# First expert's rows from two sources: an early gather of four tiles and a one-hot product from SBUF for the last, with the second gate weights loaded at another point

## The chip, the core and the metric

One core of a Trainium2 chip runs the whole program, one inference step of a decoder layer. The metric is the device time of one execution in microseconds. Inputs lie in HBM in float32, and all products are float32.

## What is computed

The reference computes one layer: RMSNorm and one input projection, two mixers side by side (gated MLP over chunks, and sparse attention with three branches), output projection with residual, then a mixture of 16 experts with residual, and a final RMSNorm. There are 512 prompt tokens and 32 sampled ones (544 rows of width 1024). The change touches the start of the experts:

```python
def _hier_moe(x, ...):                       # x: 544 x 1024, after norm2
    lg = x @ w_rg + b_rg                     # 4 groups of experts
    grp = argmax(lg); g_gate = softmax(lg)[grp]
    le = (x @ w_re + b_re) of that group     # 4 experts in it
    top_p, top_i = top_k(softmax(le), 2)     # two experts for each token
    w = g_gate * top_p / sum(top_p)
    for e in range(16):                      # hidden width 512
        h = silu(x @ w_gate[e]) * (x @ w_up[e])
        y = y + combine[:, e:e+1] * (h @ w_down[e])
    return y
```

An expert has 2 MB of gate, 2 MB of up and 2 MB of down weights, so the experts read 96 MB of weights.

## The kernel before

The program is written out by hand: one instruction list per engine (SyncE, TensorE, ScalarE, VectorE, GpSimd), ordered among each other by named semaphores. An engine takes its list strictly in order, so a wait holds all that stands behind it. Most DMAs are issued by SyncE; gathers and scatters by row index (`indirect_dma_start`) and the stores of rows by GpSimd.

**Output product and router.** The 544 rows are five tiles, taken in `ORDER` = 0, 1, 2, 4, 3 (tile 4 is the 32 sampled rows), so step r = 4 (`PT`) is a full tile of 128 rows and comes last. For each step r: `out_product(r, 0/1)` on TensorE, `residual` on VectorE gives `x2`, `rows_in_columns` turns x2 for the router, `router_parts` and `router_sum` give the logits, `chosen_of(r)` on VectorE finds the two experts (`oh` is the one-hot over experts), `positions(r)` on TensorE counts with a triangular matrix which place in its expert each token takes, `placed(r)` turns this into `in_slot`, and `tokens_in_slots(r)` accumulates in PSUM bank 1, for every expert and slot, the number of the token that sits there. Meanwhile GpSimd multiplies x2 by the norm vector into `h2` (`times_vector`, two halves), ScalarE scales it by the row's norm (`normed`), and GpSimd stores it to the HBM table `scratch_h2` (`rows_stored`, L2838) and x2 to `scratch_x3` (`raw_rows_stored`, L2821).

**Start of the experts.** After step 4, `fixed_tokens` (L2498) makes the index column of experts 0 and 1. GpSimd's `gathered(n)` (L2860) fetches the rows of expert n from `scratch_h2` into `xe[n % 2]`. TensorE's `turn_of(n)` (L1441) turns them with eight transposes into PSUM banks 0 and 1; `rows_out(n)` copies them as columns to `xeT` (ScalarE L1857 half of them, VectorE L2582 the other half); `first_of(n)` does gate and up products, `last_of(n)` the down product. Experts 0 and 1 are fixed (64 and 128 places). The other 14 are sorted by their number of tokens: `experts_weighed` (L2504) and `experts_ranked` (L2513) on VectorE write `expert_at`, from which SyncE reads which expert's weights to load third, fourth and so on (`placed`). `weights_ready` counts up to 2 when the mixing weights are there; TensorE waits for it (L1234) ahead of the experts.

**Weights.** SyncE issues them in a fixed order (L605 to L666). Gate weights go in turn to three slots, up weights to three, down weights to three; a slot is loaded again when the product that used it is counted (`g_mm`, `u_mm`, `y_mm`). Gate 0, up 0, up 1, down 0 and down 1 are loaded before the experts begin. Gate 1 goes to ring slot 4, which holds the first half of the output weights until `out_mm` counts ten. Gate 2 goes to `xr`, which holds x2, and up 2 to `tabs`, which holds h2; both have to be free first. The lines are:

```python
            sp.wait_ge(sem("out_mm"), 2 * TILES)              # L614
            gate_in_turn(1, 1)
            sp.wait_ge(sem("x2_out"), 16 * (TILES + 1))
            sp.wait_ge(sem("experts_placed"), 1)
            placed = {FIXED: expert_of(FIXED)}
            sp.wait_ge(sem("xe_in0"), 16)                     # L624
            gate_in_turn(placed[2], 2)
```

In the trace, L692 is the helper through which all matmuls go, L469 the helper of SyncE's loads.

## Time and profile before

| | before |
|---|---|
| median of three runs | 717.05 us (714.43 to 718.75) |
| profiled execution | 716.05 us, span 714.4 us |
| TensorE matmul busy | 659.5 us, 92% |
| VectorE / ScalarE / GpSimd busy | 264.0 / 188.8 / 156.3 us |
| DMA over the span | 185.61 MB, 260 GB/s |
| granted TensorE clock, mean | 0.982 |

The page gives the busy share of each engine in 40 slices of 17.9 us each (one digit is tenths, 9 is 90% or more), and under them the granted TensorE clock and the data rate:

```profile
PE   4999999999999788989999958999999999889786
POOL 0405007230143086500032411011211111201000
PEclk9999999999999999999999987999999999999999
DMA  9995238153479086602497249999999999999973
```

The experts begin in the 25th slice (from 428.6 us): from there DMA stands at 9 for fourteen slices. In the 24th TensorE has its 5, its lowest digit after the first slice, and the granted clock has an 8 and a 7 in the 24th and 25th. The change lies at this place.

### The profile page before, as it was taken

The page shows a single profiled execution, that of the slowest core. Times are in us where ns is not written, and L with a number is a line of the kernel's source. Part 1 is how long each engine was busy: PE and PEld are TensorE (multiplying, and loading weights), DVE is VectorE, ACT ScalarE, POOL GpSimd, SP SyncE. Part 2 cuts the span into 40 slices and gives each one's busy share as a digit, 9 for nine tenths or more (in the row PEclk, how much of TensorE's full clock was granted, in tenths as well). Part 3 has the DMA queues.
Part 4 walks back from the last instruction along what each step waited for, and adds up shares of the span by engine and source line. Part 5 has one row for each costly group of instructions (what it writes and reads, how often), then busy time and mean ns, then how long its engine had stood idle before and what let it go on. Part 6 is the DMA issues. An engine that isn't in the chain of part 4 may idle for free.

```text
span 714.4 us, 14840 instructions
## 1 busy us (share of the span) xinstructions
PE 659.5 (92%) x5468; PEld 420.1 (59%) x5468; DVE 264.0 (37%) x818; ACT 188.8 (26%) x465; POOL 156.3 (22%) x237
## 2 busy tenths in 40 slices
PE   4999999999999788989999958999999999889786
PEld 1476497847646355557555435865686856456432
DVE  4148220137435666765244862112111011101216
ACT  4110212212132883576333321011111010101104
POOL 0405007230143086500032411011211111201000
PEclk9999999999999999999999987999999999999999
DMA  9995238153479086602497249999999999999973
GB/s 334 380 338 189 78 128 297 46 193 119 147 234 357 38 216 165 211 1 86 154 427 301 93 177 313 403 370 395 377 371 411 354 389 379 365 380 386 368 287 136
DMA packets 56786, 185.61 MB, mean 260 GB/s; under 512 B 9021, under 2 KB 30814, under 8 KB 50562
## 3 DMA queue, kind: packets, MB, share of 16 engines
q1 hardware_dynamic: 44914, 152.54, 56.8%
q0 software_dynamic: 11792, 32.05, 14.7%
q8 instruction: 45, 0.74, 0.4%
q14 instruction: 35, 0.29, 0.1%
HBM read 172.57 MB, written 13.93 MB: 261 GB/s over the span
## 4 chain that ended last, share of the span: by engine, by line
PE 74%; DMA 14%; DVE 5%; ACT 2%; issue 2%; SPq 1%; DVEq 0%; POOLq 0%; ACTq 0%
PE ps L692 68%; DMA ring<-in_w_gate_dram 6%; DMA ring<-in_w_up_dram 5%; PE ps L941 2%; PE ps L1241 1%; SPq L429 1%; DMA ring<-in_w_in_dram 1%; DMA ring<-in_cmp_pages_dram 1%; DMA h_rows<-tabs 1%; PE ps L788 1%; PE ps L968 1%; PE ps L1114 1%; ACT tabs L1682 1%; DMA ugr<-h_rows,qbd 1%; PE ps L1045 0%
## 5 line engine op out<-in xcount | busy, mean ns | idle before, releaser
L692 PE MATMUL ps<-ring,xr 128*128 128x512 f32 (+3 forms) x640 | 140.2, 416 | 9.7 <-DMA ring<-in_w_in_dram 9.7
L692 PEld LDWEIGHTS ps<-ring,xr 128*128 128x128 f32 (+1 forms) x640 | 68.9, 152 | 73.9 <-issue 60.8
L692 PE MATMUL ps<-ring,vnr 128*32 128x128 f32 (+1 forms) x1152 | 79.8, 328 | 2.6 <-DMA ring<-in_w_gate_dram 1.5
L692 PE MATMUL ps<-ring,work 128*32 128x128 f32 (+2 forms) x512 | 71.6, 369 | 0.0
L429 POOL DMA_DIRECT2D ring<-in_sel_pages_dram x96 | 51.4, 536 | 92.2 <-issue 57.0
L692 PEld LDWEIGHTS ps<-ring,vnr 128*32 128x32 f32 (+1 forms) x1152 | 54.6, 124 | 27.7 <-issue 10.6
L2878 POOL DMA_INDIRECT x_rows<-kvn,qbd x14 | 20.6, 1469 | 199.9 <-DVE kvn L2638 60.8
L2582 DVE COPY vnr<-ps 128x256 f32<-128x256 f32 (+3 forms) x16 | 8.1, 508 | 141.9 <-PE ps L1241 141.9
L692 PE MATMUL ps<-ring 128*128 128x128 f32 (+1 forms) x512 | 60.2, 279 | 0.2 <-DMA ring<-in_cmp_pages_dram 0.2
L692 PEld LDWEIGHTS ps<-ring 128*128 128x128 f32 x512 | 59.1, 191 | 0.7 <-DMA ring<-in_cmp_pages_dram 0.4
L692 PE MATMUL ps<-ring,qT 128*32 128x256 f32 (+2 forms) x320 | 52.8, 490 | 4.4 <-DMA ring<-in_w_down_dram 3.7
L429 POOL DMA_DIRECT2D ring<-in_cmp_pages_dram x64 | 34.7, 542 | 80.6 <-PE ps L692 53.9
L692 PEld LDWEIGHTS ps<-ring,work 128*32 128x32 f32 (+1 forms) x512 | 33.6, 130 | 26.0 <-issue 24.6
L1682 ACT ACTIVATE tabs<-tabs,rt 128x128 f32<-128x128 f32 (+3 forms) x64 | 35.2, 555 | 19.6 <-DVE rt L2097 19.5
L692 PEld LDWEIGHTS ps<-ring,qT 128*32 128x32 f32 (+2 forms) x320 | 19.9, 128 | 31.0 <-issue 27.2
L2097 DVE CUSTOM_DVE_ANT_0 tabs<-ps,tabs 128x128 f32<-128x128 f32 (+3 forms) x64 | 28.1, 488 | 14.7 <-PE ps L692 13.9
L1857 ACT COPY vnr<-ps 128x256 f32<-128x256 f32 (+3 forms) x16 | 7.0, 439 | 85.1 <-PE ps L1241 85.1
L941 PEld LDWEIGHTS ps<-cst,tabs 128*128 128x128 f32 x160 | 17.2, 141 | 12.0 <-issue 7.2
L941 PE MATMUL ps<-cst,tabs 128*128 128x128 f32 x160 | 22.1, 279 | 1.8 <-ACT xr L1692 0.9
L692 PE MATMUL ps<-xr,kvn 128*64 128x128 f32 (+2 forms) x264 | 22.3, 303 | 0.3 <-DVE xr L2200 0.3
L692 PE MATMUL ps<-vnr,ring 128*128 128x128 f32 x192 | 21.8, 275 | 0.0
L692 PEld LDWEIGHTS ps<-vnr,ring 128*128 128x128 f32 x192 | 21.6, 192 | 0.0
(404 smaller groups left out, 833.4 us busy)
## 6 DMA issues: line engine op xcount, KB each, us to landing
ring<-in_w_gate_dram SPq DMA_DIRECT2D x11, 2048.0 KB, 25.5
ring<-in_w_down_dram SPq DMA_DIRECT2D x10, 2048.0 KB, 30.2
ring<-in_w_up_dram SPq DMA_DIRECT2D x9, 2048.0 KB
xr<-in_w_gate_dram SPq DMA_DIRECT2D x5, 2048.0 KB, 31.8
tabs<-in_w_up_dram SPq DMA_DIRECT2D x5, 2048.0 KB, 34.2
ring<-in_cmp_pages_dram SPq DMA_DIRECT2D x64, 128.0 KB, 5.0
ring<-in_cmp_pages_dram POOLq DMA_DIRECT2D x64, 128.0 KB, 5.3
ring<-in_w_in_dram SPq DMA_DIRECT2D x3, 2048.0 KB, 9.0
```

Source lines behind the costliest of these rows:

```text
L429: eng.dma_start(dst[:, 256 * j + part.start:256 * j + part.stop], table[bass.ds(page, 1), :, part].rearrange("o p n -> (o p) n")).then_inc ...
L692: return nc.tensor.matmul(out, lhsT, rhs, start=start, stop=stop)
L788: ins = nc.tensor.transpose(bank[:, 128 * m:128 * m + rows], src, ident[0:rows, 0:rows])
L941: ins = nc.tensor.transpose(pb[4 + g][:, at:at + P], prob[s % 3][:, g, n * k + P * m:n * k + P * m + P], ident)
L968: ins = nc.tensor.transpose(pb[7][:, P * h:P * h + P], oT[pair % 2][:, P * h:P * h + P], ident)
L1114: ins = nc.tensor.transpose(pb[2 + h][:, P * k:P * k + rows], x2[0:rows, i, W * h + P * k:W * h + P * k + P], ident[0:rows, 0:rows])
L1241: ins = nc.tensor.transpose(pb[k // 4][:, P * (k % 4):P * (k % 4) + cap], xe[par][0:cap, P * k:P * k + P], ident[0:cap, 0:cap])
L1682: A(v, v, ACT.Exp, scale=-1.0, bias=rt[:, 160 + u % 32:161 + u % 32], accum_out=rt[:, total:total + 1]).then_inc(sem("probs"), 1)
L1857: nc.scalar.copy(xeT[par][:, 0:4, 0:cap], pb[0][:, :].rearrange("p (k n) -> p k n", k=4)[:, :, 0:cap]).then_inc(sem("xt_ready"), 1)
L2097: return V.tensor_tensor_reduce(out, a, b, scale, 3.0e38, ALU.add, ALU.min, acc)
L2582: V.tensor_copy(xeT[par][:, 4:8, 0:cap], pb[1][:, :].rearrange("p (k n) -> p k n", k=4)[:, :, 0:cap]).then_inc(sem("xt_ready"), 1)
L2878: po.indirect_dma_start(scratch_x3, bass.IndirectOffsetOnAxis(slot_tokens[0:cap, n:n + 1].bitcast(U32), 0), ye[n % 2][0:cap, :], None, com ...
```

## The change

The rows of expert 0 are no longer fetched after all five steps. The token numbers of the first four steps are closed in PSUM before the last (`first_earlier` on VectorE), and GpSimd gathers these rows between its two multiplies of the last step (`first_gathered`). Slots that are empty so far stay zero; a further store writes zeros into the rows of the last tile in `scratch_h2` beforehand. On TensorE, eight products with the identity put the gathered rows as columns into banks 0 and 4 (`first_rows_gathered`), and eight products of the last tile's `h2`, still in SBUF, with a one-hot of its slots (`first_here`) add the rest (`first_rows_here`). They take the place of `turn_of(0)`. The counts of the last step move to bank 5. On VectorE, `rows_out(0)` now comes ahead of `experts_ranked`, which comes ahead of `fixed_tokens`, and one addition joins the two parts of the token table. On SyncE, gate 1 waits for the router sum of step 3, which TensorE does amid the last output product, and gate 2 no longer for `xe_in0`; up 2 waits for `xt_mm`, the count of the joined products.

```diff
+        first_here = rt[:, 372:372 + LIGHT_CAP]
+        first_found = ints[:, 28:29]
...
+        def place_counts(r):
+
+            return pb[5][:, 0:E] if r == PT else pb[6][:, E * r:E * r + E]
...
-            sp.wait_ge(sem("out_mm"), 2 * TILES)
+            sp.wait_ge(sem("logit_mm"), 2 * PT)
             gate_in_turn(1, 1)
-            sp.wait_ge(sem("x2_out"), 16 * (TILES + 1))
+            sp.wait_ge(sem("x2_out"), 16 * (TILES + 2))
             sp.wait_ge(sem("experts_placed"), 1)
...
             placed = {FIXED: expert_of(FIXED)}
-            sp.wait_ge(sem("xe_in0"), 16)
-            gate_in_turn(placed[2], 2)
             sp.wait_ge(sem("logit_mm"), 2 * TILES - 1)
             for k in range(2):
                 sp.wait_ge(sem("h2_out%d" % k), 16 * (3 - k))
+            gate_in_turn(placed[2], 2)
+            sp.wait_ge(sem("xt_mm"), 1)
             up_in_turn(placed[2], 2)
...
             def positions(r):
 
                 after(te, "in_slot", r)
+                if r:
+                    mm(place_counts(r), ones, run, True, False)
                 if r == PT:
-                    mm(pb[6][:, E * r:E * r + 2 * E].rearrange("p (k e) -> p k e", e=E), ones,
-                       run[:, None, :].to_broadcast([P, 2, E]), True, False)
-                elif r:
-                    mm(pb[6][:, E * r:E * r + E], ones, run, True, False)
+                    mm(counts, ones, run, True, False)
                 te.wait_ge(sem("onehot_ready"), r + 1)
-                ins = mm(pb[6][:, E * r:E * r + E], cst[:, C_TRI:C_TRI + P], oh[:, r, :], r == 0, r < PT)
+                mm(place_counts(r), cst[:, C_TRI:C_TRI + P], oh[:, r, :], r == 0, True).then_inc(sem("pos_mm"), 1)
                 if r == PT:
-                    ins = mm(pb[6][:, E * TILES:E * TILES + E], ones, oh[:, r, :], False, True)
-                ins.then_inc(sem("pos_mm"), 1)
+                    mm(counts, ones, oh[:, r, :], False, True).then_inc(sem("pos_mm"), 1)
...
             out_product(4, 0)
             out_product(4, 1)
+            tokens_in_slots(3)
             rows_in_columns(4, 1)
             router_parts(4)
-            tokens_in_slots(3)
             router_sum(4)
+
+            def first_bank(k):
+
+                return pb[4 * (k // 4)][:, LIGHT_CAP * (k % 4):LIGHT_CAP * (k % 4 + 1)]
+
+            def first_rows_gathered():
+
+                te.wait_ge(sem("xe_in0"), 16)
+                for k in range(KD):
+                    mm(first_bank(k), xe[0][0:LIGHT_CAP, P * k:P * k + P], ident[0:LIGHT_CAP, 0:LIGHT_CAP], k % 4 == 0, False)
+
+            def first_rows_here():
+
+                te.wait_ge(sem("h2_ready"), 2 * TILES)
+                te.wait_ge(sem("in_slot"), TILES)
+                for k in range(KD):
+                    ins = mm(first_bank(k), h2[0][:, P * k:P * k + P], first_here, False, k % 4 == 3)
+                ins.then_inc(sem("xt_mm"), 1)
+
             positions(4)
+            first_rows_gathered()
+            first_rows_here()
             tokens_in_slots(4)
             te.wait_ge(sem("weights_ready"), 2)
...
-            turn_of(0)
             first_of(0)
             turn_of(1)
             weights_in_slots()
...
+                if n == 0:
+                    nc.scalar.copy(xeT[0][:, 0:4, 0:cap], pb[0][:, 0:4 * cap].rearrange("p (k n) -> p k n", k=4)
+                                   ).then_inc(sem("xt_ready"), 1)
+                    return
...
+            def first_earlier():
+
+                dve.wait_ge(sem("slot_mm"), 1)
+                link(V.tensor_scalar(nowhere[:, 0:1], pb[1][0:CAP, 0:1], 0.0, empty_row[0:CAP, :], ALU.is_equal, ALU.mult))
+                V.scalar_tensor_tensor(out=first_found, in0=nowhere[:, 0:1], scalar=-1.0, in1=pb[1][0:CAP, 0:1],
+                                       op0=ALU.add, op1=ALU.add).then_inc(sem("part_out"), 1)
+
+            def first_last():
+
+                dve.wait_ge(sem("pos_mm"), TILES)
+                V.scalar_tensor_tensor(out=first_here, in0=slot_row[:, 0:LIGHT_CAP], scalar=place_counts(PT)[:, 0:1],
+                                       in1=oh[:, PT, 0:1].to_broadcast([P, LIGHT_CAP]), op0=ALU.is_equal, op1=ALU.mult
+                                       ).then_inc(sem("in_slot"), 1)
 
...
             residual(4, 1)
+            first_earlier()
             columns_out(4)
             norm_of(4)
             parts_out(4)
             chosen_of(4)
             dve.sem_inc(sem("weights_ready"), 1)
+            first_last()
             placed(4)
...
             def fixed_tokens():
 
-                dve.wait_ge(sem("slot_mm"), 1)
-                tokens_from(pb[1][0:CAP, 0:FIXED], slot_tokens[0:CAP, 0:FIXED], 1)
+                dve.wait_ge(sem("slot_mm"), 2)
                 link(V.tensor_copy(found_rows, pb[1][:, 0:E]))
+                link(V.tensor_tensor(found_rows, found_rows, pb[1][:, E:2 * E], ALU.add))
+                tokens_from(found_rows[0:CAP, 0:FIXED], slot_tokens[0:CAP, 0:FIXED], 1)
 
             def experts_weighed():
 
                 n = E - FIXED
+                dve.wait_ge(sem("pos_mm"), TILES + 1)
                 link(V.scalar_tensor_tensor(out=count_key, in0=cst[:, C_IE + FIXED:C_IE + E], scalar=-1.0 / 32,
...
             experts_weighed()
+            rows_out(0)
+            experts_ranked()
             fixed_tokens()
-            experts_ranked()
             dve.wait_ge(sem("rt_exp"), 2)
...
                 for n in range(2):
+                    if r == PT and n == 1:
+                        first_gathered()
                     po.wait_ge(sem("x2_ready"), 2 * r + n + 1)
                     ins = nc.gpsimd.tensor_tensor(h2[r % 2][0:rows, W * n:W * n + W], x2[0:rows, i, W * n:W * n + W],
                                                   g2[0:rows, W * n:W * n + W], ALU.mult)
@@ -2837,6 +2893,18 @@
                 po.wait_ge(sem("h2_ready"), 2 * r + 2)
                 po.dma_start(scratch_h2[i * P:i * P + rows, :], h2[r % 2][0:rows, :]
                              ).then_inc(sem("h2_out%d" % (r % 2)), 16)
+
+            last_token = po.to_reg(TOK - 1)
+
+            def first_gathered():
+
+                po.wait_ge(sem("part_out"), PT + 1)
+                po.wait_ge(sem("x2_out"), 16 * (TILES + 1))
+                for k in range(2):
+                    po.wait_ge(sem("h2_out%d" % k), 32)
+                po.indirect_dma_start(xe[0][0:LIGHT_CAP, :], None, scratch_h2,
+                                      bass.IndirectOffsetOnAxis(first_found[0:LIGHT_CAP, :].bitcast(U32), 0),
+                                      bounds_check=last_token, oob_is_err=False).then_inc(sem("xe_in0"), 16)
 
             po.wait_ge(sem("vectors_in"), 48)
             for r in range(PT):
@@ -2848,14 +2916,13 @@
                 nc.gpsimd.memset(xe[k], 0.0).then_inc(sem("iota"), 1)
             po.wait_ge(sem("iota"), 5)
             po.dma_start(scratch_x3[TOK:TOK + CAP, :], xe[0][0:CAP, :]).then_inc(sem("x2_out"), 16)
+            po.dma_start(scratch_h2[P * ORDER[PT]:P * ORDER[PT] + P, :], xe[0]).then_inc(sem("x2_out"), 16)
             times_vector(PT)
...
             def experts(b):
 
-                gathered(E * b)
+                if b:
+                    gathered(E * b)
                 gathered(E * b + 1)
                 gathered(E * b + 2)
```

## Rows read from the trace of the kernel before

**Rows 1.** Busy time in stretches; the first line names the columns

```profile
core 0: us, PE busy (x) PEld busy (x) DVE busy (x) ACT busy (x) POOL busy (x), PEclk, DMA share, GB/s
395.00:431.30 36.30, 24.74 (x146) 14.57 (x145) 26.51 (x108) 9.45 (x19) 12.39 (x14) 0.87 0.38 131
431.30:470.00 38.70, 37.06 (x294) 28.94 (x298) 10.47 (x40) 4.38 (x7) 4.03 (x4) 0.90 0.99 386
470.00:477.00 7.00, 7.00 (x160) 5.40 (x152) 0.00 (x0) 0.49 (x1) 0.33 (x1) 1.00 0.99 283
477.00:600.00 123.00, 122.97 (x1208) 83.05 (x1200) 18.41 (x35) 14.69 (x29) 19.90 (x16) 1.00 1.02 385
600.00:688.90 88.90, 77.95 (x867) 44.92 (x856) 14.78 (x27) 11.07 (x22) 10.15 (x8) 0.98 0.96 361
```

**Rows 2.** Chain of work that ended last: start us, us, what

```profile
421.04 5.66 DMA h_rows<-tabs
...
427.56 3.61 DMA ugr<-h_rows,qbd
...
655.16 33.68 DMA ring<-in_w_up_dram
```

**Rows 3.** Timeline of SyncE's DMA issues: start us, us, what

```profile
416.73 0.33 SPq L469 DMA_DIRECT2D ring<-in_w_gate_dram  x1
...
431.32 0.35 SPq L469 DMA_DIRECT2D xr<-in_w_gate_dram  x1
...
471.97 0.33 SPq L469 DMA_DIRECT2D xr<-in_w_gate_dram  x1
```

**Rows 4.** SyncE's waits, 415 to 433 us: for whom, us in total, times, longest

```profile
SPq L617 <- DVE ints L2521: 10.8, 1, 10.8
SPq L469 <- DMA ugr<-h_rows,qbd: 2.7, 1, 2.7
```

**Rows 5.** Timeline of all engines, 408 to 433 us, selected lines

```profile
408.50 1.12 DVE L2428 TENSOR_TENSOR rt<-rt 128x16 f32<-128x16 f32 x1
...
412.18 0.96 PE L692 MATMUL ps<-ksT,qT 128*128 128x16 f32 x8
...
417.51 1.27 POOL L2830 TENSOR_TENSOR tabs<-xr,tabs 128x512 f32<-128x512 f32 x1 [7.92 <-DVE xr L2365]
...
419.59 1.15 ACT L1785 ACTIVATE tabs<-tabs,small 128x1024 f32<-128x1024 f32 x1
...
422.79 1.04 PE L692 MATMUL ps<-rt,cst 128*128 128x16 f32 x4 [2.12 <-DVE rt L2411]
...
426.46 0.36 DVE L2516 TENSOR_TENSOR work<-work,cst 128x196 f32<-128x196 f32 x1
...
427.56 1.01 POOL L2866 DMA_INDIRECT ugr<-h_rows,qbd  x1 [5.40 <-DMA h_rows<-tabs]
...
427.65 0.17 DVE L2521 CAST ints<-work 128x14 int32<-128x14 f32 x1
...
428.98 0.33 DVE L2573 TENSOR_TENSOR ksT<-ksT,rt 128x160 f32<-128x160 f32 x1
...
431.30 1.08 PE L1241 MATMUL ps<-cst,ugr 64*128 64x64 f32 x8 [5.47 <-DMA ugr<-h_rows,qbd]
...
432.42 0.42 DVE L2582 COPY vnr<-ps 128x256 f32<-128x256 f32 x1 [3.11 <-PE ps L1241]
...
432.90 10.03 PE L692 MATMUL ps<-ring,vnr 128*64 128x256 f32 x64 [0.52 <-DVE vnr L2582]
```

**Rows 6.** Stretches around the start of the experts, for the granted clock (columns as above)

```profile
418.40:421.80 3.40, 1.75 (x24) 1.41 (x24) 2.23 (x11) 2.39 (x3) 1.14 (x3) 0.99 0.84 352
421.80:431.30 9.50, 2.07 (x8) 1.89 (x9) 6.28 (x33) 0.56 (x3) 2.43 (x3) 0.50 0.58 207
431.30:438.90 7.60, 7.08 (x38) 4.28 (x40) 3.24 (x17) 1.66 (x2) 0.98 (x1) 0.50 0.93 345
```

**Rows 7.** GpSimd's gathers of rows, all sixteen

```profile
DMA to landing us min/median/max: 4.6/12.3/16.7
```

More of the change, by code:

```diff
@@ L2561, in overflow_flag, with rows_out @@
                 dve.wait_ge(sem("flag_ready"), 1)
+            def rows_out(n):
+                par = n % 2
+                dve.wait_ge(sem("xt_mm"), n + 1)
+                after(dve, "u_mm", n - 1)
+                cap = cap_of(n)
+                if n == 0:
+                    V.tensor_copy(xeT[0][:, 4:8, 0:cap], pb[4][:, 0:4 * cap].rearrange("p (k n) -> p k n", k=4)
+                                  ).then_inc(sem("xt_ready"), 1)
+                    return
+                V.tensor_copy(xeT[par][:, 4:8, 0:cap], pb[1][:, :].rearrange("p (k n) -> p k n", k=4)[:, :, 0:cap]
+                              ).then_inc(sem("xt_ready"), 1)
             experts_weighed()
+            rows_out(0)
+            experts_ranked()
             fixed_tokens()
-            experts_ranked()
             dve.wait_ge(sem("rt_exp"), 2)
@@ L2655, in experts @@
             def experts(b):
-                rows_out(E * b)
+                if b:
+                    rows_out(E * b)
                 if b == 0:
@@ L2856, in _ @@
             po.wait_ge(sem("slots_ready"), 1)
-            last_token = po.to_reg(TOK - 1)
             def gathered(n):
@@ L2881, in experts @@
             def experts(b):
-                gathered(E * b)
+                if b:
+                    gathered(E * b)
                 gathered(E * b + 1)
```

28 lines of the change are left out of this document (11 added, 17 removed).

## The prediction

> **What bounds the kernel now.** I read the busy times in stretches first [rows 1]. From 431.3 us to 688.9 us, the sixteen experts, the DMA engines are busy for a share of 0.96 to 1.02 at 361 to 386 GB/s, with one weak spot from 470 to 477 us (283 GB/s). TensorE is also busy nearly throughout until 600 us, and only then has room: 77.95 of 88.9 us. So two chains run side by side, and the stream of weights is the one that arrives last: the chain of waits ends on an up-weight load that needed 33.68 us from issue to landing, because it stood behind other slabs [rows 2]. What moves the end is therefore the time at which the stream becomes continuous, and not TensorE's first expert by itself. Before 431.3 us there is much room: DMA share 0.38, TensorE 24.74 of 36.3 us [rows 1].
>
> SyncE's issues show what starts the stream [rows 3]. Gate 1 goes at 416.73 us. Gate 2 (slot `xr`) goes at 431.32 us, and up 2 and up 3 follow at once. By SyncE's waits [rows 4] it waited 10.8 us for the ranking of the experts and then 2.7 us for the gathered rows of expert 0. So the gather, and not the ranking, releases gate 2, and taking it out of that wait can be worth at most 2.7 us. Behind the gather stands this chain: scaling on ScalarE at 419.59, store of the rows at 421.04 (5.66 us to landing), indirect DMA at 427.56 (3.61 us) [rows 2, 5], eight transposes at 431.30, copies at 432.42, first product of expert 0 at 432.90 [rows 5].
>
> **The change part by part.** *Gate 1* goes in the last output product instead of behind it. Its bytes move within a stretch where the DMA has 0.62 of its time free [rows 1], and expert 1 needs them only after expert 0 (432.90 + 10.03 us [rows 5]). Cover is large on both sides: 0.
>
> *The early gather.* VectorE's two small operations lie between the residual and a copy that waits for TensorE: 0. GpSimd now issues the gather between its two multiplies of the last tile. The index is ready near 418 us (the second multiply, which follows the residual, starts at 417.51 us [rows 5]), the issue takes 1.01 us as at 427.56, and the second multiply then ends near 420.7 instead of 418.78. ScalarE's scaling and both stores slide about 1.1 us (store 422.2 instead of 421.04, landed by about 428.4). The gathered rows land near 418.1 + 3.61 = 422 us. Nothing waits for either as long as the steps below are later; if that cover goes, the stores hold gate 2 until about 428.4 us. The moved multiply could also hold up VectorE: one small operation took 1.12 us beside such a multiply [rows 5], where its like take under 0.2. I bound this at 0 to 1.0 us, and take 0, since the operations that fall beside it now read PSUM as the residual and copies do, which show nothing of the kind. The extra zero store and VectorE's one-hot (one operation of 64 columns) lie in idle time: 0.
>
> *The joined products.* Eight transposes (1.08 us) go; eight products of gathered rows with the identity and eight of the last tile's rows with the one-hot come. A float32 product is two instructions here, so 32 instructions, each with a 128x128 weight load. The trace has two prices for such instructions with few columns [rows 5]: eight in 0.96 us at the upper clock (0.12 us each), four in 1.04 us at the lower (0.93/4, so 0.23 us each when the last one's tail is left out). The granted clock before the experts is 1.00 until 421.8 us, then 0.50 until 438.9 us, so the lower of the two levels (1.2 and not 2.4 GHz) [rows 6]; before it fell, TensorE was busy 1.75 of 3.4 us with small instructions. The change adds nothing in that stretch and leaves the wait for the last one-hot (to 422.79 us), so I let it fall again. The chain is then: positions end at 423.83 (422.79 + 1.04), 32 x 0.23 + 0.25 = 7.6 us of products, columns ready at 431.4 us. Before it was 432.4 us. Only 1.0 us is won, as the two halves of the product run one behind the other at half clock. With the upper clock it would be 423.3 + 3.9 = 427.2 us.
>
> TensorE page of the Trainium skill ("TensorE: Matmul & The Clock Gate", section "LDWEIGHTS (loading the stationary operand)"): a weight load takes its columns divided by 1.2 in nanoseconds, however many rows, so 107 ns here and also for the 64 gathered rows; by it the products would take an estimated 3.4 us and the result would be that of the second rival. The trace agrees at the upper clock (0.12 us) and not at the lower (0.23 us).
>
> *What moved behind them on VectorE.* This is the step that I think decides. `rows_out(0)` now stands ahead of `experts_ranked`, of `fixed_tokens` and of the weights. What is queued behind its wait for the columns is: the ranking, on which SyncE's gate 2 waits; the token table, on which GpSimd's gather for expert 1 waits; and `weights_ready`, which TensorE still waits for ahead of expert 0. Before, all three were done by 429.31 us, while TensorE still waited for its rows. Now, from 431.4 us:
> - copy of columns 0.05 + 0.42 us: 431.9;
> - ranking, the span from 426.46 to 427.82 us [rows 5] = 1.36 us: 433.3. SyncE needs about 0.85 us from there (before: 427.82 us, then its 2.7 us wait began at 431.17 - 2.7 = 428.5, plus 0.15 to issue). Gate 2: **434.1 us, 2.8 us later than now**;
> - token table, four operations of about 0.2 us: 434.1;
> - weights, from 427.82 to 429.31 us [rows 5] = 1.5 us: 435.6. Expert 0 starts at **435.7 us, 2.8 us later than now**.
>
> *The gather for expert 1* is issued at 434.3 instead of right behind the first. It then runs beside gate 2 and up 2. Landing of these gathers took 4.6 us at least, 12.3 median, 16.7 at most [rows 7]; the 4.6 was of the idle queue, so I take 12.3: 446.6 us. TensorE wants it at the end of expert 0, now 442.9 us, then between 443 and 446. So TensorE is at this point 3 to 4 us later than now.
> The same gather also brings up to 128 rows x 4 KB = 0.52 MB into the busy stream: at 386 GB/s [rows 1] 1.4 us at most.
>
> DMA page of the Trainium skill ("DMA: Bandwidth & Descriptors", section "Queues, rings and completion order"): an engine takes turns between the queues that have work. By equal turns, 0.52 MB would come at half of 386 GB/s in an estimated 2.7 us, and expert 1 would not wait. The landing median speaks against it; by that rule the sum would lose only TensorE's part, and keep the stream's.
>
> **The sum.** The stream starts 2.8 us later and carries up to 1.4 us more: +2.8 to +4.2. Against this, from 470 to 477 us it moved 283 and not 386 GB/s, a hole of 7 x 103/386 = 1.9 us in which it had caught up with TensorE's releases (gate 5 at 471.97 [rows 3]). If TensorE is less late than the stream, part of the hole closes; by the gather row it is about as late. I take +3.0 us, range +2 to +4.2. The profiled execution took 716.05 us (span 714.4), 1.0 below the median 717.05 of three runs (714.43 to 718.75). So 719.1 beside the profiled run, and **720.0 us** beside the median.
>
> **The rivals.**
> 1. *The late gather starves TensorE (slower).* One mechanism, the gather for expert 1 behind the slabs. If it lands as late as the slowest row, 434.3 + 16.7 = 451 us, TensorE is 8 us late for expert 1, its releases come late, and the hole at 470 to 477 us grows from 1.9 by 8 - 3 = 5 us at most. Half of it gives +3.0 + 2.5 = 722.5 us. It decides from a landing later than about 447 us. For it: the queue then holds two slabs, 4.2 MB or 10.9 us at 386 GB/s. Against: the 12.3 median.
> 2. *The clock does not fall, or late (about the same).* Columns at 427.2 us, gate 2 at 429.9 (-1.4), expert 0 at 431.5 us and at full pace. The stream wins 1.4 and carries 1.4 more, TensorE is ahead and closes some of the hole: -1.0, 716.0 us. For it: TensorE now has products directly behind the positions. Against: the fall was over by then.
> 3. *The change does what it says (faster).* If the products cost at the lower clock what the transposes cost, 1.08/8 = 0.135 us each, columns stand at 428.4 us at 32 instructions and at 426.2 at 16. Gate 2 is then held by the stores at 428.4 us, -2.5 beside 431.32, the 0.52 MB gather falls mostly ahead of the stream, and the closed hole gives up to 1.9 more. -3.8, so 713.2 us. Against: the 1.04 us row.
>
> **How the numbers follow.** Forecast 0.47, rival 1 0.16, rival 2 0.21, rival 3 0.16. What a measurement of this kernel can tell from no change is about 0.5%, 3.6 us: same is 713.5 to 720.6 us. Forecast's own range is 719 to 721.3 and splits 0.34 same, 0.13 slower. Faster: 0.15 of rival 3, with 0.01 of rival 2: 0.16. Same: 0.34 + 0.20 + 0.01 = 0.55. Slower: 0.13 + 0.16 = 0.29. The range takes all but the outer parts of rivals 1 and 3: 713.2 to 723.0 us.
>
> **What would show each step.** In the profile after: gate 1 issued near 411 us, and the first gather near 418; the row of identity and one-hot products directly ahead of expert 0, 32 instructions, at 0.23 us (forecast) or 0.12 us (rival 2); granted clock 0.50 from about 422 us; VectorE idle for TensorE ahead of the first column copy for 5 to 6 us; SyncE's gate 2 later than 431.3 by 2 to 3 us and released by the ranking; TensorE waiting for `weights_ready` ahead of expert 0, and for a gather ahead of expert 1's transposes; the last up slab landing near 692. I am wrong if gate 2 goes before 431 us, or if it goes later and the last up slab still lands at 689, which would mean that the stream is not what sets the end.

## The result, and the profile after

The median of seven runs is 724.28 us (721.39 to 726.73) after, and 716.67 us (714.43 to 718.75) before, which is the median of seven runs now and was 717.05 us over the first three. The ratio is 1.0117, with a 95% interval of 1.0084 to 1.0150; here and below the ratio is estimated from the single runs and is not the quotient of the two medians. The change makes the kernel slower by 7.6 us. The profiled execution took 726.33 us with a span of 724.6 us, 10.2 us above that of before; it is 2 us above its own median, so the trace shows somewhat more of the loss than a typical run has.

From the page of after, the granted clock and the DMA share in 40 slices of 18.1 us:

```profile
PEclk9999999999999999999999966899999999999999
DMA  9996148153479177403595429979999999999973
```

Before, the clock dipped in two slices at the start of the experts and the DMA stood at 9 from the 25th slice on. Now the clock has 6, 6 and 8 in the 24th to 26th slice, and the DMA has a 7 in the 27th (from 471 us).

The timeline of after around the last step, in order: start, duration, engine and line, operation, how many, and the idle time before it with its releaser.

```profile
418.86 1.06 POOL L2905 DMA_INDIRECT ugr<-h_rows,ints  x1 [8.44 <-DVE ints L2472]
...
419.62 1.63 DVE L2402 TENSOR_TENSOR small<-small 128x1 f32<-128x1 f32 x1
...
419.94 1.28 POOL L2886 TENSOR_TENSOR tabs<-xr,tabs 128x512 f32<-128x512 f32 x1
...
424.54 1.03 PE L699 MATMUL ps<-rt,cst 128*128 128x16 f32 x4 [1.74 <-DVE rt L2441]
...
425.50 3.67 PE L699 MATMUL ps<-cst,ugr 64*128 64x64 f32 x16
...
429.10 3.67 PE L699 MATMUL ps<-rt,tabs 128*128 128x64 f32 x16
...
432.88 0.42 DVE L2618 COPY vnr<-ps 128x256 f32<-128x256 f32 x1 [5.36 <-PE ps L699]
...
434.40 0.17 DVE L2569 CAST ints<-work 128x14 int32<-128x14 f32 x1
...
435.44 0.35 SPq L476 DMA_DIRECT2D xr<-in_w_gate_dram  x1
...
436.12 1.06 POOL L2933 DMA_INDIRECT ugr<-h_rows,qbd  x1 [11.64 <-DVE qbd L2532]
...
436.93 10.10 PE L699 MATMUL ps<-ring,vnr 128*64 128x256 f32 x64 [3.38 <-DVE ksT L2635]
...
483.43 0.33 SPq L476 DMA_DIRECT2D xr<-in_w_gate_dram  x1
```

The first three answer to the rows of the last step in [rows 5]. The rest answers to the second half of [rows 5]: the joined products are the two groups of sixteen ahead of 432.88 us. VectorE waits 5.36 us for them ahead of its first copy, the ranking follows at 434.40, gate 2 (SyncE) at 435.44 instead of 431.32 [rows 3], and the gather for expert 1 at 436.12, where before it went right behind the one for expert 0 (at 428.87 us, and landed in 4.6 us). Gate 5, the next load into `xr`, goes at 483.43 us instead of 471.97 [rows 3].

What SyncE (395 to 440 us; first fence) and TensorE (430 to 720 us; second fence) waited for: us in total, how often, and the longest wait. L624 is the wait for the ranking:

```profile
SPq L624 <- DVE ints L2569: 22.1, 1, 22.1
```

```profile
PE ps L699 <- DVE ksT L2635: 3.4, 1, 3.4
...
PE ps L1268 <- DMA ugr<-h_rows,qbd: 2.5, 1, 2.5
```

The chain of work that ended last (start, duration, what), between 430 and 480 us in after, then the same place in before. It answers to [rows 2]:

```profile
436.12 13.35 DMA ugr<-h_rows,qbd
...
449.52 1.74 PE ps L1268 x8
451.26 4.30 PE ps L699 x20
455.56 0.51 PE ps L1354 x2
456.07 16.25 PE ps L699 x128
472.31 0.66 PE ps L1268 x8
```

```profile
442.93 1.02 PE ps L1241 x8
443.96 2.34 PE ps L692 x20
446.30 0.27 PE ps L1327 x2
446.56 14.29 PE ps L692 x128
460.86 0.66 PE ps L1241 x8
```

After now has the gather in the chain, 13.35 us from issue to landing. Behind it stand the same groups of products with the same counts, but they take 1.74, 4.30, 0.51 and 16.25 us where before they took 1.02, 2.34, 0.27 and 14.29.

Last, busy times in stretches (the columns as in [rows 1]): three of after, and the one of before that [rows 1] does not have:

```profile
431.30:470.00 38.70, 32.82 (x214) 28.32 (x215) 10.39 (x48) 3.22 (x5) 2.97 (x3) 0.72 0.87 332
470.00:477.00 7.00, 6.56 (x45) 3.85 (x44) 0.83 (x2) 0.83 (x2) 0.00 (x0) 1.00 0.96 396
477.00:485.00 8.00, 7.32 (x114) 5.58 (x116) 2.41 (x6) 0.82 (x2) 2.47 (x2) 1.00 0.48 102
```

```profile
477.00:485.00 8.00, 8.00 (x39) 3.89 (x27) 0.77 (x3) 0.95 (x2) 0.00 (x0) 1.00 1.01 428
```

In this trace these lines add up to the loss. Before moved 386 x 38.7 + 283 x 7 = 16.9 MB to 477 us [rows 1], after 332 x 38.7 + 396 x 7 = 15.6 MB: 1.3 MB less, 3.4 us at 386 GB/s. From 477 to 485 us before moved 3.4 MB and after 0.8 MB: 2.6 MB less, 6.8 us. Together 10.2 us, which is the difference of the spans. The 3.4 us are themselves a balance: 5.4 us lost up to 470 us (332 instead of 386 GB/s), mostly because the stream starts late, less 2.0 us won back from 470 to 477 us, where before had its own small hole. The 6.8 us are a new hole, in which SyncE waits for a slot and TensorE is behind.

### The profile page after: what moved, and what is told of

The parts are those of the page before. It is cut to its first block, busy times and chain, and to the rows that moved or that the text cites. A ratio compares the mean times of both kernels' runs of the same rounds, so it can differ in the third digit from the quotient of the medians.

```text
span 724.6 us, 14899 instructions
## 1 busy us (share of the span) xinstructions
PE 669.5 (92%) x5494; PEld 432.6 (60%) x5494; DVE 265.9 (37%) x822; ACT 188.8 (26%) x465; POOL 157.0 (22%) x238
## 4 chain that ended last, share of the span: by engine, by line
PE 73%; DMA 15%; DVE 6%; ACT 2%; issue 2%; SPq 1%; DVEq 0%; POOLq 0%; ACTq 0%
PE ps L699 67%; DMA ring<-in_w_gate_dram 6%; DMA ring<-in_w_up_dram 5%; PE ps L948 2%; DMA ugr<-h_rows,qbd 2%; DMA ring<-in_cmp_pages_dram 1%; PE ps L1268 1%; SPq L436 1%; DMA xr<-in_xT_dram 1%; PE ps L795 1%; PE ps L975 1%; PE ps L1121 1%; ACT tabs L1708 1%; PE ps L1052 0%; DVE vnr L2274 0%
## 5 line engine op out<-in xcount | busy, mean ns | idle before, releaser
L699 PE MATMUL ps<-ring,xr 128*128 128x512 f32 (+3 forms) x640 | 138.4, 413 | 9.5 <-DVE xr L1998 9.5
L699 PE MATMUL ps<-ring 128*128 128x128 f32 (+1 forms) x512 | 61.7, 283 | 1.8 <-DMA ring<-in_cmp_pages_dram 1.8
L699 PE MATMUL ps<-vnr,ring 128*128 128x128 f32 x192 | 23.8, 290 | 0.0
L699 PEld LDWEIGHTS ps<-vnr,ring 128*128 128x128 f32 x192 | 23.7, 207 | 0.0
```

What stands on the lines that cost most here:

```text
L699: return nc.tensor.matmul(out, lhsT, rhs, start=start, stop=stop)
```

## The experiments

The theory that I set out with after the result (T): the gather for expert 1 sits in the queue behind the weights, TensorE runs out of work, its clock falls once more, and the slots come free late. The rival (S): the stream starts late because gate 2 waits for the ranking. A third (V): VectorE loses time beside GpSimd's moved multiply. (The expectations call T theory G, and V theory C.) Six kernels start from after (e), six from before (b). Names of lines are those of after or before. Each result gives the median, the ratio to before with its 95% interval, and the profiled span. The kernel before stood at a median of 714.45 us beside e1, e3, e4 and b3, at 716.04 us beside e2, e6, b2 and b4, and at 715.68 us beside e5, b1, b6 and b7; its profiled span is 714.4 us throughout. Two profiled executions differ before the experts begin, too: the last residual ("last residual" in the table below), which none of these edits is meant to move, starts anywhere from 415.29 to 418.72 us. Where a difference of one or two microseconds matters, I give the time from there.

**e1: the ranking ahead of the copy.**

```diff
             experts_weighed()
-            rows_out(0)
             experts_ranked()
+            rows_out(0)
             fixed_tokens()
```

> The changed kernel with one step of VectorE moved: the ranking (experts_ranked) ahead of the first column copy. Gate 2 should then be issued near 430.5 us instead of 435.4; the token table, and with it the gather for expert 1, stays behind the columns (issue 436 us). Theory S, the start of the weight stream sets the end: 4 to 5 us faster than the changed kernel, ratio to the kernel before 1.004 to 1.006. Theory G, the late gather for expert 1 sets it (TensorE waits for it, its clock falls, its releases come late): no gain or a small loss, ratio 1.010 to 1.014, since the gather now meets a longer queue and the landing takes 13 us or more.

721.56 us, 1.0101 (1.0062 to 1.0141), span 723.0 us. Stretches, and TensorE's transposes of expert 1:

```profile
431.30:470.00 38.70, 34.30 (x227) 29.93 (x227) 9.32 (x44) 3.22 (x5) 2.97 (x3) 0.73 1.00 381
470.00:477.00 7.00, 5.88 (x40) 3.16 (x40) 1.85 (x3) 1.16 (x2) 0.00 (x0) 1.00 0.39 131
477.00:485.00 8.00, 8.00 (x124) 5.91 (x122) 1.40 (x5) 0.49 (x1) 2.47 (x2) 1.00 0.55 120
```

```profile
448.47 1.36 PE L1268 MATMUL ps<-cst,ugr 128*128 128x128 f32 x8 [1.91 <-DMA ugr<-h_rows,qbd]
```

Gate 2 went at 430.40 us, 5 us sooner than in after and sooner than in before. The stream is full again until 470 us (381 GB/s), and then falls to 131 and 120 GB/s: the sum to 485 us is 16.6 MB, against 16.4 in after and 20.3 in before. What was loaded sooner was waited for later. S alone has fallen. This is what theory G expected. The gather was issued at 435.85 us, TensorE waited 1.9 us for it, and the transposes behind it took 1.36 us for eight.

**e4: the token table ahead of the copy, the ranking still behind.** On TensorE `tokens_in_slots(4)` goes between the two halves of the joined products.

```diff
             first_rows_gathered()
-            first_rows_here()
             tokens_in_slots(4)
+            first_rows_here()
...
             experts_weighed()
+            fixed_tokens()
             rows_out(0)
             experts_ranked()
-            fixed_tokens()
```

> The changed kernel with the token table (fixed_tokens) ahead of the first column copy and the last tokens_in_slots between the two halves of the joined products; the ranking stays behind the columns. The gather for expert 1 should be issued near 431.5 us, ahead of gate 2 (436 us), and land in about 4 to 5 us. Theory G: TensorE doesn't wait ahead of expert 1's transposes, the second stretch at the lower clock goes, 5 to 7 us faster than the changed kernel, ratio 1.002 to 1.005. Theory S: gate 2 is as late as before or 0.5 us later, so nothing is won, ratio 1.010 to 1.013.

717.75 us, 1.0033 (1.0007 to 1.0060), span 718.8 us.

```profile
437.78 8.56 PE L699 MATMUL ps<-ring,vnr 128*64 128x256 f32 x64 [3.27 <-DVE ksT L2635]
446.27 1.09 PE L1268 MATMUL ps<-cst,ugr 128*128 128x128 f32 x8
447.19 2.50 PE L699 MATMUL ps<-ksT,qT 128*128 128x16 f32 x20
```

```profile
431.30:470.00 38.70, 34.32 (x266) 27.95 (x267) 12.08 (x50) 4.39 (x7) 2.98 (x3) 0.88 0.87 329
470.00:477.00 7.00, 7.00 (x114) 5.28 (x111) 1.39 (x5) 0.49 (x1) 2.48 (x2) 1.00 1.04 397
477.00:485.00 8.00, 8.00 (x99) 4.96 (x96) 0.75 (x2) 0.32 (x2) 0.00 (x0) 1.00 1.02 351
```

The opposite of e1: gate 2 is the latest of all (437.11 us), expert 0 starts later than in after, and yet it is 5.8 us faster in the span. The gather went at 432.77 us, ahead of the slabs; TensorE did not wait, the clock did not fall again (eight transposes 1.09, twenty products 2.50 us), and the hole is gone. What is left of the loss is the late start: 18.3 MB to 485 us, 2.0 MB or 5.2 us short, for a span 4.4 us longer. The last residual was 1.7 us later here than in before, so of TensorE's 3.4 us at expert 1 only 1.7 are the edit's, and of gate 2's 5.8 us 4.1. The intervals of e4 and of after do not overlap: the early gather removes most of the loss.

**e3: the gather for expert 0 behind both multiplies.**

```diff
                 for n in range(2):
-                    if r == PT and n == 1:
-                        first_gathered()
...
             times_vector(PT)
+            first_gathered()
             rows_stored(PT)
```

> The changed kernel with GpSimd's early gather behind both multiplies of the last tile instead of between them. The multiply then starts as before, right behind the residual, and VectorE's small addition (1.63 us beside the multiply in the changed kernel, 0.15 us in the kernel before) should take 0.15 us again. Theory C, that collision is on the path: 1.0 to 1.6 us faster than the changed kernel, ratio 1.009 to 1.010. Rival: the gather 1.2 us later eats this up, or the late gather for expert 1 does: ratio 1.011 to 1.012.

723.12 us, 1.0124 (1.0062 to 1.0185), span 721.4 us. VectorE's row beside the multiply, and TensorE's at expert 1:

```profile
418.42 0.15 DVE L2402 TENSOR_TENSOR small<-small 128x1 f32<-128x1 f32 x1
...
447.81 1.17 PE L1268 MATMUL ps<-cst,ugr 128*128 128x128 f32 x8 [3.86 <-DMA ugr<-h_rows,qbd]
```

The addition took 0.15 instead of 1.63 us and everything behind it came 1.7 us sooner (gate 2 at 433.78 us); 1.2 of these 1.7 us were there already at the last residual (416.38 against 417.57), so 0.5 us are the edit's. The median shows nothing of it (the profiled span is 3.2 us shorter than that of after, but after's was one of its slowest runs): TensorE then waited 3.9 us for the gather instead of 2.5. The collision V is real, and it is not the cause.

**b3: only VectorE's new order, on before.** Ranking, table and weights are already ahead there; here the ranking and the weights go behind the copy, while the table stays ahead. TensorE's wait for the weights moves behind `turn_of(0)`, and a new semaphore `found` lets it overwrite the token table only when VectorE has read it.

```diff
-            te.wait_ge(sem("weights_ready"), 2)
...
+            te.wait_ge(sem("found"), 1)
             turn_of(0)
+            te.wait_ge(sem("weights_ready"), 2)
             first_of(0)
...
                 link(V.tensor_copy(found_rows, pb[1][:, 0:E]))
+                dve.sem_inc(sem("found"), 1)
...
             experts_weighed()
             fixed_tokens()
+            rows_out(0)
             experts_ranked()
```

> The kernel before, with its own gather and transposes, and only VectorE's order of the change: first column copy ahead of the ranking and of the mixing weights; TensorE waits for the weights between the transposes and expert 0. The token table stays ahead, so both first gathers go as before. Gate 2 should be issued near 435.2 us instead of 431.3 and expert 0 start near 435.9 instead of 432.9. Both theories: 3 to 4 us slower than before, ratio 1.004 to 1.006, if what is late at the start is late at the end. If the hole of 1.9 us at 470 to 477 us can be closed, 1.001 to 1.003. What the changed kernel loses beyond this is the joined products' and the gather's.

716.66 us, 1.0028 (0.9997 to 1.0059), span 714.9 us. Gate 2 went at 433.29 us (+2.0) and expert 0 at 434.03 us (+1.1); the gather for expert 1 still went early, at 427.15 us, and gate 5 went where it does in before, at 471.87 us. The last residual was 1.5 us earlier here than in before; measured from it gate 2 went 3.4 us later, expert 0 began 2.6 us later, near the 3.9 and 3.0 us that I expected, and expert 1 1.4 us later. I had expected 1.004 to 1.006 from that; the ratio is lower. A late ranking without a late gather costs at most a small part.

**e6: TensorE kept at work while the gather is on its way.** After, with six products of 384 columns that nobody reads, between expert 0 and the transposes of expert 1.

```diff
             first_of(0)
+            for _ in range(6):
+                mm(pb[5][:, 0:384], ident, cst[:, 0:384])
             turn_of(1)
```

> The changed kernel with six products of the identity with 384 constant columns, into a PSUM bank that nobody reads, between the first product of expert 0 and the transposes of expert 1, so in TensorE's wait for the gather (2.5 us idle in the changed kernel); its outputs stay the same. Theory K, the second fall of the clock, which follows that idle stretch (granted 0.50 from 449.5 to 459.7 us), is a large part of the loss: the clock stays at 1.00 there, transposes, slot weights and the first product of expert 1 win 4 to 5 us, 4 to 5 us faster than the changed kernel, ratio 1.004 to 1.007. Rival W, only the lateness of the gather counts, or the stream does: no gain, ratio 1.010 to 1.013.

721.71 us, 1.0102 (1.0028 to 1.0176), span 718.1 us.

```profile
444.78 4.14 PE L699 MATMUL ps<-cst 128*128 128x384 f32 x12
448.76 1.04 PE L1268 MATMUL ps<-cst,ugr 128*128 128x128 f32 x8
```

```profile
442.70:449.50 6.80, 6.80 (x39) 4.20 (x36) 0.00 (x0) 0.00 (x0) 0.00 (x0) 1.00 1.03 391
449.50:459.70 10.20, 10.20 (x78) 10.15 (x77) 3.99 (x16) 0.59 (x1) 0.91 (x1) 0.83 1.01 367
```

```profile
442.70:449.50 6.80, 4.33 (x40) 2.48 (x36) 0.00 (x0) 0.38 (x1) 0.00 (x0) 0.98 1.04 401
449.50:459.70 10.20, 10.18 (x48) 10.11 (x49) 3.98 (x16) 0.58 (x1) 0.91 (x1) 0.51 1.00 350
```

(The stretches are first of e6, then of after.) Expert 0 ended sooner here, at 444.78 us, since the clock came back earlier in it, and the products took that time up again: expert 1 began 0.8 us sooner than in after (448.76 against 449.52). What differs is the clock, 0.83 instead of 0.51 from 449.5 to 459.7 us: it fell all the same, without a gap before it, but only for the stretch 452 to 456. Gate 5 went at 479.43 instead of 483.43 us and the span is 6.5 us shorter. In the medians it is less, 721.71 us, and the intervals of this ratio and of after's overlap. The two profiled executions lie at opposite ends of their runs (e6's is its fastest, after's its second slowest), so part of the 6.5 us is chance. The profile shows gate 5 4.0 us sooner, 0.8 of which is the earlier start of expert 1; the ratio of 1.0102 lies where the expectation had its rival W, no gain. What the second fall costs in the time is not shown.

**e2: all three ahead of the copy.** After, with TensorE's order of e4 and `rows_out(0)` behind the weights on VectorE.

```diff
             experts_weighed()
-            rows_out(0)
             experts_ranked()
             fixed_tokens()
...
                             ).then_inc(sem("weights_ready"), 1)
+            rows_out(0)
```

> The changed kernel with all three pieces (ranking, token table, mixing weights) ahead of the first column copy, and the last tokens_in_slots between the halves of the joined products. Gate 2 near 430.5 us, gather for expert 1 issued near 432 beside it and landing near 444, expert 0 starting near 435. Theory G (the gather's landing and the clock after it decide): about as the kernel with only the gather early, which was 1.0033, a little better since expert 0 starts 3 us sooner and worse if TensorE waits for the gather: 0.999 to 1.004. Theory S (the stream's start adds to that): 5 us less than 1.0033, ratio 0.996 to 0.998.

714.97 us, 0.9972 (0.9936 to 1.0008), span 714.4 us. **e5** is e2 with the edit of e3:

> The changed kernel with all three pieces of VectorE ahead of the first column copy and, on GpSimd, the early gather behind both multiplies. VectorE's small addition should take 0.15 us again, and all that follows the last one-hot come 1 to 1.9 us earlier than in the kernel with the order alone (0.9972): expert 0 near 433.7 us. Theory P: 0.994 to 0.997. Rival: the gather for expert 1 now lands too late and TensorE waits for it: 0.997 to 1.001.

714.44 us, 0.9990 (0.9957 to 1.0022), span 712.6 us. Expert 0 and the transposes of expert 1 on TensorE in e5:

```profile
432.62 9.86 PE L699 MATMUL ps<-ring,vnr 128*64 128x256 f32 x64 [0.56 <-issue]
442.40 1.09 PE L1268 MATMUL ps<-cst,ugr 128*128 128x128 f32 x8
```

In both the gather goes early (at 432.97 and 430.24 us), TensorE waits for nothing at expert 1, and the loss is gone. Measured from the last residual, expert 1 and gate 5 stand in both where they stand in before, within 0.2 us. So it is the order on VectorE, and not the joined products, that costs. e5 also has the addition at 0.15 us and gate 2 at 428.20 us, and stands level with before all the same; neither the gain that I expected (0.994 to 0.997) nor the wait of the rival is there.

**b2 and b1: the two earlier loads alone, on before.**

```diff
-            sp.wait_ge(sem("xe_in0"), 16)
-            gate_in_turn(placed[2], 2)
             sp.wait_ge(sem("logit_mm"), 2 * TILES - 1)
             for k in range(2):
                 sp.wait_ge(sem("h2_out%d" % k), 16 * (3 - k))
+            gate_in_turn(placed[2], 2)
```

> The kernel before with one part of the change alone: gate 2 no longer waits for the gathered rows of expert 0. Gate 2 should be issued near 428.7 us instead of 431.3. Theory S: the stream is 2.6 us earlier, 1 to 2.6 us faster, ratio 0.996 to 0.999. Theory G: the two first gathers now run beside gate 2, expert 0 starts later by up to several us, and nothing or less than nothing is won, ratio 1.000 to 1.008.

713.16 us, 0.9985 (0.9948 to 1.0022), span 711.6 us, gate 2 at 427.44 us.

```diff
-            sp.wait_ge(sem("out_mm"), 2 * TILES)
+            sp.wait_ge(sem("logit_mm"), 2 * PT)
             gate_in_turn(1, 1)
```

> The kernel before with one part of the change alone: gate 1 issued in the middle of the last output product instead of behind it. All theories: it lands in idle DMA time and isn't wanted before 442 us; no difference, ratio 0.998 to 1.002, gate 5 at the same place relative to the last residual.

716.15 us, 0.9996 (0.9966 to 1.0027), span 716.1 us, gate 1 at 411.09 us. Neither can be told from before. In b2 gate 2 went 3.9 us sooner and the profiled span was 2.8 us shorter; 1.2 us of both were there at the last residual already, and the ratio shows nothing. In b1 and b2 expert 0 happened to run in 8.45 and 8.47 us instead of 10.03, since the clock came back earlier in it; no edit of theirs touches that, so a single trace is uncertain by some 1.6 us at expert 1.

**b4, b6, b7: the clock, on before.** Products that nobody reads ahead of the last one-hot and of the transposes of expert 0: five and twelve in b4; three and seven in b6, where the seven stand ahead of the wait for `weights_ready`. b7 is b6 with the edit of b2.

```diff
                 if r == PT:
+                    for _ in range(5):
+                        mm(pb[5][:, 0:384], ident, cst[:, 0:384])
...
+            for _ in range(12):
+                mm(pb[5][:, 0:384], ident, cst[:, 0:384])
             turn_of(0)
```

> The kernel before with products of the identity with 384 constant columns in TensorE's two waits ahead of expert 0: five ahead of the wait for the last one-hot, twelve ahead of the transposes of expert 0, into a PSUM bank that nobody reads; outputs stay the same. The granted clock should stay at 1.00 where it was 0.50 from 421.8 to 438.9 us, so expert 0's first product takes 7.1 instead of 10.0 us and TensorE is 3 us earlier for expert 1. Theory T, the stretch up to 477 us is paced by TensorE's releases, and the stream had a hole of 1.9 us there: 1.5 to 3 us faster, ratio 0.996 to 0.998. Rival S, the stream alone sets the end: no change, 0.999 to 1.001.

722.14 us, 1.0102 (1.0035 to 1.0169), span 718.9 us. I had made them too long: the twelve ran from 430.89 us for 9.57 us, and expert 0 began at 441.62 us. The five ran past the one-hot as well, to about 425.1 us. As an experiment it serves another end: gate 2 went nearly as in before (432.63 us), the stream was full until 470 us (380 GB/s), and only TensorE was late, 5.8 us at expert 1.

```profile
443.00:470.00 27.00, 27.00 (x234) 23.02 (x232) 6.15 (x27) 2.04 (x4) 1.88 (x2) 1.00 1.01 394
470.00:477.00 7.00, 5.88 (x90) 4.03 (x90) 2.69 (x6) 0.68 (x1) 2.48 (x2) 1.00 0.59 179
```

From 470 to 477 us the stream fell to 179 GB/s, gate 5 went at 477.78 us, and the span grew by 4.5 us. The clock stood at 1.00 from 443 to 470 us, so it did not fall a second time, and the ratio is the 1.0102 of e6 all the same. A late TensorE alone makes the hole, and a second fall of the clock is not needed for it.

> The kernel before with unread products of the identity with 384 constant columns in TensorE's waits, sized by their measured 0.64 us each: three (1.9 us) ahead of the wait for the last one-hot, seven (4.5 us) ahead of the wait for the mixing weights, so that they end before the gathered rows land. Theory P, TensorE's releases up to gate 5 pace the end (span = issue of gate 5 + 241 us in the ten kernels so far, within 2.5): the clock stays up, the first product of expert 0 takes about 7.2 us, gate 5 goes 3 us earlier than in the kernel before, and up to 3 us are won, ratio 0.995 to 0.998. Rival S, once the hole of 1.9 us at 470 to 477 us is closed the stream is the bound: 0.997 to 0.999.

715.31 us, 0.9992 (0.9963 to 1.0021), span 713.4 us.

```profile
433.78 7.13 PE L692 MATMUL ps<-ring,vnr 128*64 128x256 f32 x64 [0.52 <-DVE vnr L2587]
```

> The same kernel, and gate 2 no longer waits for the gathered rows of expert 0 (issue 2.6 us earlier). Theory P: no different from the one with the short products alone, 0.995 to 0.998. Rival S, the stream is the bound once TensorE is early: 2 us faster than that one, 0.992 to 0.996.

714.30 us, 0.9986 (0.9954 to 1.0018), span 711.7 us. In b6 expert 0 runs in 7.13 instead of 10.03 us [rows 5] and TensorE is 2 us ahead at expert 1, and nothing can be measured of it (3.0 us ahead, measured from the last residual). b7 waits 1.9 us for the gather at expert 1 and its clock falls again for a short stretch. Both ratios lie just above the 0.995 to 0.998 that I had given theory P. A TensorE that is early is worth nothing; one that is late costs.

One table over these kernels, all from the profiled executions (start of the last residual, issue of gate 2, transposes of expert 1, issue of gate 5, span; us):

| kernel | last residual | gate 2 | expert 1 | gate 5 | span |
|---|---|---|---|---|---|
| before | 416.74 | 431.32 | 442.87 | 471.97 | 714.4 |
| after | 417.57 | 435.44 | 449.52 | 483.43 | 724.6 |
| e1 | 417.98 | 430.40 | 448.47 | 482.38 | 723.0 |
| e3 | 416.38 | 433.78 | 447.81 | 481.72 | 721.4 |
| e6 | 417.01 | 434.88 | 448.76 | 479.43 | 718.1 |
| b4 | 416.30 | 432.63 | 448.68 | 477.78 | 718.9 |
| e4 | 418.45 | 437.11 | 446.27 | 475.37 | 718.8 |
| e2 | 418.72 | 430.93 | 444.88 | 473.98 | 714.4 |
| e5 | 416.44 | 428.20 | 442.40 | 471.50 | 712.6 |
| b3 | 415.29 | 433.29 | 442.77 | 471.87 | 714.9 |
| b2 | 415.50 | 427.44 | 440.06 | 469.17 | 711.6 |
| b7 | 415.50 | 428.00 | 440.79 | 471.52 | 711.7 |
| b6 | 417.69 | 432.01 | 440.84 | 469.94 | 713.4 |
| b1 | 416.52 | 430.91 | 440.86 | 469.96 | 716.1 |

From gate 5 to the end it is 238.7 to 246.1 us. The five kernels whose medians lie above 721 us (after, e1, e3, e6, b4) are the five in which expert 1 starts at 447.8 us or later. By gate 2 alone e1 would have to be among the fast ones and e4 the slowest. Measured from the last residual and against before, expert 1 is late by 5.8 us in after, 6.3 in b4, 4.4 in e1, 1.7 in e4, 1.4 in b3 and 0.0 in e2, and early by 3.0 in b6; the ratios are 1.0117, 1.0102, 1.0101, 1.0033, 1.0028, 0.9972 and 0.9992. Gate 5 is late or early by the same as expert 1, within 0.1 us, in every kernel whose clock does not fall in between.

## Why the prediction was wrong

I forecast 720.0 us in 713.2 to 723.0; the median was 724.28 us.

*What held.* The joined products ran at the lower clock, 32 of them in 7.27 us (425.50 to 432.77), so 0.23 us each, and not at 0.12 as in the second rival or 0.135 as in the third. The copy waited 5.36 us for them. VectorE's new order was the step that decides, in the order named: gate 2 released by the ranking (+4.1 us, forecast +2.8), the gather for expert 1 late (436.12 us, 13.35 us to landing, forecast 12.3), expert 0 behind `weights_ready` (+4.0 us, forecast +2.8). Gate 1 sooner cost and brought nothing (b1).

*A term that was mis-sized: VectorE beside the multiply.* I bounded this term at 0 to 1.0 us and took 0, since what falls beside it reads PSUM. But the small addition L2402 reads two operands in SBUF, and it took 1.63 us beside GpSimd's 1.28; with the multiply out of the way it took 0.15 (e3). SBUF page of the Trainium skill ("SBUF — State Buffer", section "Terms"): VectorE and GpSimd share a pair of ports that one of them holds for its whole instruction, and the other is blocked. The trace agrees in that the addition ends at 421.25 us, right with the multiply at 421.22, although by its record it had begun 0.32 us ahead of it. The row of 1.12 us that I had in [rows 5] was the same case. That is 1.5 us of lateness for the addition. The positions ended at 425.57 us instead of the 423.83 of my sum, 1.74 us later. The last residual was 0.8 us later in this execution (417.57 against 416.74), for which I have no cause. Of the other 0.9 us the collision is about half: from the residual to the start of the positions it is 6.05 us in before, 6.97 in after, and still 6.50 in e3 and 6.51 in e5, where the addition took 0.15 us. The rest shows in the copy L2417 ahead of the router sum, which in e3 waited 0.93 us for TensorE instead of 0.31, and stays unexplained. Less the 0.3 us by which the products were shorter than my 7.6, this is the gap between +2.8 and +4.1 us. By e3 and e5 none of it could be seen in the time.

*The step that failed: that the stream's start sets the end.* I wrote that TensorE's first expert is not what moves the end, and let the sum go by gate 2 and the bytes, with TensorE only closing the hole from 470 to 477 us. What the runs show in its place: the end is set by the later of two chains, and they lie so close at gate 5 that a few microseconds on TensorE turn them over. From e1 and b4: with the stream on time and TensorE 5.6 and 5.8 us late at expert 1, the span grew by 8.6 and 4.5 us. From e4: with TensorE 3.4 us late and gate 2 5.8 us late, by 4.4 us. From b6: with TensorE 2.0 us early, by nothing that can be measured. In after TensorE was 6.6 us late at expert 1 and 11.5 us at expert 2, and the hole came at 477 to 485 us, 6.8 us of the 10.2.

*A step that was not there: the clock falls a second time.* My sum had the late gather as 3 to 4 us at expert 1, without consequences. It was 6.6 us: the gather was issued 1.8 us after the 434.3 of my sum and took 13.35 and not 12.3 us, which makes 449.5 of 446.6. That was a matter of size. But after the 2.5 us of idle time TensorE was granted 0.51 from 449.5 to 459.7 us, and four groups of products took (1.74 - 1.02) + (4.30 - 2.34) + (0.51 - 0.27) + (16.25 - 14.29) = 4.9 us more. Before had this once, at the start of the experts [rows 6], and I carried it over, but did not ask where else TensorE would idle. 4.0 + 0.1 + 2.5 + 4.9 = 11.5 us is the whole lateness at expert 2. So it is in this trace. What the fall costs in the time is open: e6 is 4.0 us ahead at gate 5 in the profile but has the ratio 1.0102, b4 has the same ratio with no second fall, and both intervals overlap with that of after. The lateness of TensorE at expert 1 is enough for a loss of this size.

*The rivals.* The first had the mechanism, the gather behind two slabs starving TensorE, and the right place for the loss, the hole. Its price was too small in two ways: I let it begin only from a landing at 447 us and took half of the growth (722.5 us). The landing was 449.5 us, and TensorE's lateness at gate 5 was more than the wait, as the 4.0 us of expert 0 and the fall of the clock went with it. I also gave it a chance of only 0.16, although 447 us lay 0.4 us behind the landing of my own sum (446.6), well within what the rows of landings leave open [rows 7]. The second and the third, that the clock stays up and that the change does what it says, fell with the 0.23 us. But e2 and e5 show what is left of the third once VectorE's order is undone: 0.9972 and 0.9990, level with before. I have no version that is faster than before by more than the measurement can tell.

*My own conditions.* I named as proof against me that gate 2 goes late and the last up slab lands at 689 us; it landed at 699.1 (666.16 + 32.98). The test was passed and the model was wrong all the same: a late TensorE moves the same slab. A condition that both theories meet proves neither.

## What to carry to other kernels

Where a weight stream and an engine run level, ask of each reordering what it does to the later one, and price both chains at the next slot that the stream needs back, not at the place of the edit. Issue small gathers ahead of large loads, even when their user comes much later: here 13.35 us went by between issue and landing of the rows of expert 1, against 4.6 us before, when the same gather went ahead of the slabs. Before reading a microsecond between two profiles, take off what differs ahead of the edit; here it was up to 3.4 us. When an instruction that waits is moved up in an engine's list, go through all that it now holds back, and through who needs it while it waits.

## What the runs showed of the hardware that I had not expected

- An addition on 128x1 elements took 1.63 us beside GpSimd's multiply and 0.15 us without it. The size of the operation does not bound what such a collision costs.
- In after the granted clock fell again after 2.5 us in which TensorE waited for the gather, at the end of ten microseconds of products, and it stayed at 0.5 although TensorE was busy for 10.18 of the next 10.2 us. It did the same in e1 and e3 (waits of 1.9 and 3.9 us), and for a shorter stretch in b7 (1.9 us; 0.83 from 440 to 450 us). In e4, e2, e5, b4 and b6, without such a wait, it stood at 1.00 from 441 to 460 us. But in e6 it fell for a short stretch with no gap before it, so the wait is not the whole condition, and how long a fall lasts is open.
- An unread float32 product of 384 columns takes 0.69 us (4.14 us for six in e6, with the granted clock at 1.00). The twelve of b4 took 9.57 us, so they held expert 0 back by more than the faster clock gave.
